# Retention layer: the input projection as seven products per pair of tiles, the attention in items of one head and 256 tokens, the out projection in one piece

## The reference, cut to what matters

```python
q, k, v, g = jnp.split(h @ w_in, ...)            # h 1024x1024, w_in 1024x6144
q, k = rope(q), rope(k) * dk ** -0.5             # 4 heads, dk 256, dv 512
for each chunk of tokens:                        # decay per head
    scores = q k^T * intra
    o      = scores v + (q state) * q_decay
    state  = state * chunk_decay + (k * k_decay)^T v
o = o * rsqrt(mean(o * o) + eps)                 # per head and token
y = (o * silu(g)) @ w_out                        # w_out 2048x1024
```

## Time and profile before

| what | value |
|---|---|
| median of three runs | 2658.11 us |
| the profiled execution's own time | 2658.08 us |
| its span | 2656.2 us |
| PE busy | 2616.3 us, 98% of the span |
| DVE busy | 1378.0 us, 52% |
| POOL busy | 1500.1 us, 56% |
| ACT busy | 869.6 us, 33% |
| granted TensorE clock | 0.998 |
| HBM read, written | 132.81 MB, 5.24 MB |

### The profile page before, as it was taken

One profiled execution on the slowest core, in us unless ns is written; L12 is line 12 of the kernel. 1 busy time (PEld: TensorE's weight loads), 2 busy tenths in 40 slices (PEclk: granted clock), 3 DMA queues, 4 the chain that ended last, 5 costly groups with the idle time before them and its releaser, 6 DMA issues.

```text
span 2656.2 us, 34669 instructions
## 1 busy us (share of the span) xinstructions
PE 2616.3 (98%) x11833; PEld 2159.5 (81%) x11833; DVE 1378.0 (52%) x1740; ACT 869.6 (33%) x1456; POOL 1500.1 (56%) x1334
## 2 busy tenths in 40 slices
PE   8999999999999999999999999999999999999998
PEld 6888888888888788888888788888877888888887
DVE  8333322323325856465563647375678364655644
ACT  4130120121124533333333524234256233333324
POOL 4314323322433478888788644363453788887865
PEclk9999999999999999999999999999999999999999
DMA  4102112111111111211212111111111112112122
GB/s 144 41 28 64 44 32 61 48 36 52 48 44 44 43 54 48 63 47 47 63 53 66 36 49 45 36 56 40 45 56 38 59 48 63 47 47 63 47 68 83
DMA packets 173780, 139.44 MB, mean 52 GB/s; under 512 B 9200, under 2 KB 143472, under 8 KB 173680
## 3 DMA queue, kind: packets, MB, share of 16 engines
q1 hardware_dynamic: 171584, 133.46, 16.8%
q10 hardware_dynamic: 2096, 4.62, 0.5%
HBM read 132.81 MB, written 5.24 MB: 52 GB/s over the span
## 4 chain that ended last, share of the span: by engine, by line
PE 86%; DVE 8%; issue 3%; ACT 2%; DMA 0%; DVEq 0%; SPq 0%; ACTq 0%
PE ps L978 28%; PE ps L982 28%; PE ps L981 28%; DVE residual L2786 2%; DVE f_h_lo L2530 1%; DVE uc L2877 1%; PE ps L1318 0%; DVE h_lo L2326 0%; PE ps L1227 0%; DVE scratch L2307 0%; ACT gate_buf L1628 0%; DVE uc L2871 0%; DVE f_act L2742 0%; DMA residual<-in_x 0%; DVE gate_buf L2882 0%
## 5 line engine op out<-in xcount | busy, mean ns | idle before, releaser
L745 POOL TENSOR_TENSOR f_w_lo<-f_raw,f_w_hi 128x512 fp32r<-128x512 f32 x306 | 434.4, 1423 | 253.1 <-ACT f_w_hi L1837 94.4
L703 POOL TENSOR_TENSOR small<-w_raw 128x1 f32<-128x1 f32 x200 | 54.9, 274 | 792.8 <-PE ps L978 782.3
L978 PE MATMUL ps<-f_h_hi,f_w_hi 128*128 128x512 f32 x1232 | 481.1, 391 | 3.7 <-DVE f_h_lo L2530 2.4
L982 PE MATMUL ps<-f_h_hi,f_w_lo 128*128 128x512 f32 x1232 | 479.6, 389 | 0.0
L981 PE MATMUL ps<-f_h_lo,f_w_hi 128*128 128x512 f32 x1232 | 479.5, 389 | 0.0
L978 PEld LDWEIGHTS ps<-f_h_hi,f_w_hi 128*128 128x128 f32 x1232 | 231.3, 188 | 57.5 <-issue 4.3
L982 PEld LDWEIGHTS ps<-f_h_hi,f_w_lo 128*128 128x128 f32 x1232 | 231.3, 188 | 48.1
L981 PEld LDWEIGHTS ps<-f_h_lo,f_w_hi 128*128 128x128 f32 x1232 | 231.3, 188 | 47.0
L714 POOL TENSOR_TENSOR w_lo<-w_raw,w_hi 128x512 fp32r<-128x512 f32 x190 | 258.7, 1362 | 15.2
L745 POOL TENSOR_TENSOR f_w_lo<-f_sum,f_w_hi 128x512 fp32r<-128x512 f32 x142 | 220.4, 1553 | 60.9 <-ACT f_w_hi L1837 60.9
L978 PE MATMUL ps<-h_hi,w_hi 128*128 128x512 f32 x632 | 249.0, 394 | 0.9 <-DVE h_lo L2277 0.6
(11 more groups left out here) (365 smaller groups left out, 4985.9 us busy)
## 6 DMA issues: line engine op xcount, KB each, us to landing
f_raw<-in_ffn_w_gu SPq DMA_DIRECT2D x176, 256.0 KB, 3.9
w_raw<-in_ret_w_in SPq DMA_DIRECT2D x96, 256.0 KB, 2.8
f_raw<-in_ffn_w_down SPq DMA_DIRECT2D x88, 256.0 KB, 2.9
w_raw<-in_lru_w_in SPq DMA_DIRECT2D x48, 256.0 KB, 2.9
w_raw<-in_ret_w_out SPq DMA_DIRECT2D x32, 256.0 KB, 2.6
w_raw<-in_lru_w_out SPq DMA_DIRECT2D x24, 256.0 KB, 2.8
residual<-in_x SPq DMA_DIRECT2D x8, 512.0 KB, 7.7
out_y<-residual SPq DMA_DIRECT2D x7, 512.0 KB, 2.7
```

Of the source, the lines that this page charges most:

```text
L703: nc.gpsimd.tensor_tensor(small[:, 62:63], col, col, ALU.subtract)
L745: nc.gpsimd.tensor_tensor(lo, src, hi.bitcast(F32), ALU.subtract).then_inc(f_wready, 1)
L978: m = nc.tensor.matmul(o, l_hi, r_hi, start=start, stop=False, skip_group_check=onto)
L982: return nc.tensor.matmul(o, l_lo, r_hi, start=False, stop=stop, skip_group_check=onto)
```

## The change: what it does

The loop over heads goes. In its place:

1. **Norm and first pair.** `norm_by_halves` and `norm_by_halves_act` get a form for `layer == RET` (-1), which makes the seven forms of the normed input right at the start of the program, and `first_products(RET)` does the first two units of the input projection in the order of `PLACES_FIRST`.
2. **Input projection.** 24 units of two 128-feature tiles each (`IN_ORDER`: per head v, v, q, k, and the eight units of g at the end), seven products each, in PSUM banks 0 to 3. All results are features by tokens. DVE turns q and k (`turned`, 12 operations of 128x512 per unit), ACT applies Silu to g; SP writes each unit's four 128x512 parts to HBM (`spill`).
3. **Attention by items.** 16 items (head, 256 tokens), each of four parts, placed between products: part m follows product 35 + 19m/10 (`PARTS`). Part 0: k turned and scores; 1: v turned back to tokens by features; 2: outputs and state; 3: outputs turned. Its operands are read from HBM (`load_qk`, `load_v`), its outputs, normed and turned, are written there (`store_o`). It uses banks 4 to 7.
4. **Out projection.** `load_rows` reads o and g by head and half of the tokens, DVE multiplies, ACT and DVE split; 64 weight pieces, each 12 matmuls, first all of tokens 0 to 511, then 512 to 1023. x is read from HBM again (`x_again`), as `X` serves as work space meanwhile.

The core of it:

```diff
+IN_UNITS = 24
+OUT_UNITS = 64
+IN_ORDER = ([(kind, h, i) for h in range(HEADS) for kind, i in (("v", 0), ("v", 1), ("q", 0), ("k", 0))]
+            + [("g", h, i) for h in range(HEADS) for i in range(2)])
+ITEM_PARTS = 4
+FIRST_PART = 35
+PARTS = {}
+for m in range(ITEM_PARTS * ITEMS):
+    PARTS.setdefault(FIRST_PART + m * 19 // 10, []).append((m // ITEM_PARTS, m % ITEM_PARTS))
...
-            head(0, True)
-            with pe.Fori(1, HEADS - 1) as h:
-                head(h, False)
-            head(HEADS - 1, False, True)
+            for i in range(4):
+                transposes(RET, i)
+            pe.wait_ge(cols_ready, 1)
+            first_products(RET)
+            pe.wait_ge(ident_ready, 3)
+            for r in range(2, IN_UNITS):
+                for p in range(PRODUCTS):
+                    in_product(r, p)
+                    for it, part in PARTS.get(PRODUCTS * r + p, ()):
+                        if part == 0:
+                            keys_and_scores(it)
+                        elif part == 1:
+                            values_turned(it)
+                        elif part == 2:
+                            outputs_and_state(it)
+                        else:
+                            outputs_turned(it)
+            out_rows()
             ffn(0)
```

PE's products of a unit, and what they wait for:

```diff
+            def in_product(r, p):
+                j, form, before = PRODUCTS * r + p, H_OF[p], 0 if r == 2 else r - 1
+                if p == 0:
+                    if IN_ORDER[before][0] in "qk":
+                        pe.wait_ge(r_rope, 12 * turned_no(before) + 2)
+                    else:
+                        pe.wait_ge(r_c11, plain_no(before) + 1)
+                elif p < 4:
+                    pe.wait_ge(f_ev, in_ev(before, (None, E_C21, E_C12, E_T6)[p]))
+                elif p == 4:
+                    pe.wait_ge(f_t, r + 1)
+                else:
+                    pe.wait_ge(f_ev, in_ev(r, (E_T5, E_T7)[p - 5]))
```

```diff
+            def projected():
+                angles()
+                turns(4096.0)
+                whole_turns()
+                for i in range(3):
+                    less(i, 4096.0)
+                first_pair_up()
+                turn_arguments()
+                for r in range(2, IN_UNITS):
+                    turn = IN_ORDER[r][0] in "qk"
+                    for p in range(PRODUCTS):
+                        j = PRODUCTS * r + p
+                        if p in (1, 2, 3):
+                            in_sum(r, p - 1)
+                        elif p == 4 and turn:
+                            turned(r, 0, 2)
+                        elif p == 5:
+                            in_less(r, E_C21, j + 1)
+                            if turn:
+                                turned(r, 2, 6)
+                        elif p == 6:
+                            in_less(r, E_C12, j + 1)
...
+                        if p == 6 and turn:
+                            turned(r, 6, 12)
```

ACT's order at the start, in `norm_by_halves_act(RET)`:

```diff
+                    root(0, 4, turn_a)
+                    for j in range(3):
+                        w_round_first(c, j)
+                    act.wait_ge(cols_ready, 1)
+                    act.wait_ge(n_sq, 4)
+                    for k in FOUR:
+                        from_bank(H_hi[:, h_cut(H_Q11, k)], k)
+                        from_bank(t_q[:, t_cut(k)], k)
+                    for k in FOUR:
+                        from_bank(H_hi[:, h_cut(H_Q21, k)], 4 + k)
+                        from_bank(r3(4 + k), 4 + k)
+                    first_term(c, 0, AT_FIRST)
+                    unit(3)
+                    first_term(c, 1, AT_FIRST)
+                    for s in range(4, SB):
+                        act.wait_ge(x_in[s], 16)
+                        square_rows(s, 0, t_b[:, t_cut(s - 4)])
+                    scaled_last()
```

and DVE's and ACT's work around the first out rows (in unit 23, p counts its products):

```diff
+                        if r == IN_UNITS - 1:
+                            if p in (2, 3):
+                                rows_gated(p - 2)
+                            elif p == 5:
+                                rows_lower(0)
+                rows_lower(1)
...
+            def out_ahead(end, done=[3]):
+                for w in range(done[0], end):
+                    if w in ROWS_AT:
+                        rows_upper(ROWS_AT[w])
+                    out_round(w)
```

More of the change, by code:

```diff
@@ L391, in hn_at @@
         def hn_at(order, what, k, layer):
-            return layer * len(order) + order.index((what, k)) + 1
+            return (layer + 1) * len(order) + order.index((what, k)) + 1
         def h_cut(form, k):
@@ L578, in pair @@
                     for i, src in enumerate(tile_rows_of(f, 1)):
+                        if first and layer == 0:
+                            sp.wait_ge(f_wready, n.units - 4 + i + 1)
                         if not first and i == 0:
@@ new lines, in values_turned @@
+            def values_turned(it):
+                c = it % N_CHUNKS
+                pe.wait_ge(r_vin, 16 * (it + 1))
+                pe.wait_ge(r_mask, it + 1)
+                if c < N_CHUNKS - 1:
+                    pe.wait_ge(r_kt, chunks_before(it) + 1)
+                for blk in range(CHUNK):
+                    for d in range(4):
+                        m = nc.tensor.transpose(bank(4 + blk, d * P, P),
+                                                v_raw[:, d * ITEM + blk * P:d * ITEM + (blk + 1) * P], ident[:])
+                    m.then_inc(r_vt, 1)
@@ L1936, in norm_by_halves_act @@
-                for s in range(4, SB):
-                    added(act, n, 1, s)
-                    square_rows(s, 1, r3(s - 4))
-                root(4, SB, turn_b)
-                act.wait_ge(n_rstd, turn_b)
-                for half in range(2):
-                    for s in (6, 7):
-                        at = s * D + half * 512
-                        nc.scalar.activation(xn_at(half, s), X[:, at:at + 512], ACT.Copy,
-                                             scale=rstd[:, s:s + 1]).then_inc(hx_act, 1)
@@ L1946, in norm_by_halves_act, with junk, scaled_last @@
-                act.wait_ge(n_sq, sq + 16)
-                first_term(c, 0, AT_FIRST)
-                from_sum(H_T1, 0, t_a, "T1")
-                q_12(0)
-                q_12(1)
-                from_sum(H_T1, 1, t_a, "T1")
-                unit(3)
-                first_term(c, 1, AT_FIRST)
+                def junk(s):
+                    return t(s) if s < 3 else dk[:, 0:512]
+                def scaled_last():
+                    root(4, SB, turn_b)
+                    act.wait_ge(n_rstd, turn_b)
+                    for half in range(2):
+                        for s in (6, 7):
+                            at = s * D + half * 512
+                            nc.scalar.activation(xn_at(half, s), X[:, at:at + 512], ACT.Copy,
+                                                 scale=rstd[:, s:s + 1]).then_inc(hx_act, 1)
@@ new lines, in item_turned, with rows_upper @@
+            def item_turned(it):
+                for blk in range(CHUNK):
+                    act.wait_ge(r_ot, 2 * it + blk + 1)
+                    nc.scalar.activation(o_raw[:].rearrange("p (d n) -> p d n", d=4)[:, :, blk * P:(blk + 1) * P],
+                                         bank(4 + blk).rearrange("p (d n) -> p d n", d=4), ACT.Copy).then_inc(r_oc, 1)
+            def rows_upper(q):
+                half, h = divmod(q, HEADS)
+                act.wait_ge(r_gated, q + 1)
+                act.wait_ge(f_mm, PROJECTED + 20 + 4 * h if half else PROJECTED - (0 if h >= 2 else 4))
+                nc.scalar.activation(rows_hi[h][:], o_and_g(q)[0], ACT.Copy).then_inc(r_rh, 1)
@@ L2510, in adds @@
                         e = by_halves(n, nh, half * 4 + i)
-                        add(e, i + (4 * nh if half == 0 else 0), half * 4 + i, nh)
+                        if layer == 0:
+                            out_add(half, nh, i)
+                        else:
+                            add(e, i + (4 * nh if half == 0 else 0), half * 4 + i, nh)
                 def seen(*what):
@@ L2610, in first_tiles_up, with out_rows @@
+            def out_rows():
+                for q in (2, 3):
+                    rows_gated(q)
+                    rows_lower(q)
+                for i in range(4):
+                    out_add(0, 0, i)
+                for q in (4, 5, 6):
+                    rows_gated(q)
+                    rows_lower(q)
+                for i in range(4):
+                    out_add(0, 1, i)
+                rows_gated(7)
+                rows_lower(7)
             def first_tiles_up(layer):
```

1433 lines of the change are left out of this document (789 added, 644 removed).

## The result

The changed kernel takes 2667.59 us (median of 6 runs, 2667.25 to 2669.59). The kernel before took 2657.86 us beside it (6 runs, 2656.07 to 2658.49). The ratio is 1.0039, its 95% interval 1.0026 to 1.0052: slower by 9.7 us, where 11.6 us less was forecast.

The account below looks back on a forecast made before the run. PE was taken to bound the retention layer from end to end. Terms -51.6 + 25.3 + 8 + 6.7 = -11.6 took 2658.1 to 2646.5 us; own range 2636 to 2655, chance 0.50; whole range 2620 to 2675.

Parts of the forecast that it names:

- Products and v turned back: Input projection: 288 fewer matmuls save 64.9 us, 128 more transposes of v cost 13.3; PE's work falls by 51.6 us.
- the split parts' slow pace: Rival, chance 0.10: v transposes at 0.23 us each instead of 0.104 add 12 us net and eat the saving; 2658.
- The start: Norm and first pair: PE waits 42.6 us against 17.3 before in the whole layer; adds 25.3, bounds 10 and 35.
- the walk: Step-by-step timing of the start: T1 at 37.4, (0,6) at 77.3 behind eight angle operations, last products end at 85.3.
- The second rival: q and k units: DVE becomes the bound if two-SBUF-input operations take 1.48 us or more; 2668, chance 0.20.
- The middle: Between the products from unit 2 on: PE waits 8 us over 64 attention parts, bounds 0 and 30.
- 0.7 us of lateness: Attention parts: the longest step is some 0.7 us late behind the four rope operations of product 5.
- From input to out projection: PE waits 3 us for row 0's lower part and 3.7 behind row 2; together 6.7, bounds 0 and 15.
- The clock: Half clock after idling: 1.8 us added for the hole before (0,6); two shorter holes about 1.7 each, not summed.

Follow-up runs that it names:

- POOL almost idle: Changed kernel with POOL's weight sums and lower parts on 32 of 512 columns from unit 2 of the input projection on; 2651.04 us.
- The narrow turning: Changed kernel with each of DVE's 96 rope operations on 32 of 512 columns; 2654.6 us.
- the moved turning: Changed kernel with squares early, angles spread, rows 2 and 3 later, plus each turned unit's last six turning operations put behind the next unit's value parts; 2644.22 us.
- angles behind: Changed kernel with DVE's eight angle operations put behind the sums of the first pair instead of ahead; 2664.61 us.
- row 2 later: Changed kernel with ACT making the upper parts of out projection rows 2 and 3 before weights 7 and 10 instead of 5 and 9; 2661.74 us.
- all four together: Changed kernel with squares early, angles spread, rows 2 and 3 later and the last six turning operations behind the value parts; 2644.22 us.
- the filled kernel: Changed kernel with 45 unread matmuls of 128x512 put in PE's hole before product (0,6) of the first pair; 2663.94 us.

## Why the prediction was wrong

The sign was wrong although each place was named. Two prices of the sum failed: that of DVE's operations beside POOL, in the start and between the products, and that of PE's half clock behind a wait, which was counted once. The sum was -51.6 + 25.3 + 8 + 6.7 = -11.6. Measured by the same parts it is -51.6 + 33.6 + 15.8 + 10.7 + 0.7 = +9.2, beside 9.3 between the spans. The start is 95.44 - 44.5 of work - 17.3 waited before. The middle is 692.04 - 95.44 = 596.6 less a content of 580.8: 22 units' 1848 matmuls and the 432 of values and state at 0.2252, 54.0 of small ones and 13.3 of transposes. The out projection is 879.03 - 692.04 less 768 matmuls and 32 transposes, 176.3. The 0.7 is the FFN pair.

*Products and v turned back: right.* With POOL almost idle the whole middle takes 581.4 us where the content is 580.8, a wait of 1.5 at its end included. The transposes of v run at 8 in 0.79 us, as counted. So the 51.6 us are saved. Of the rivals, the split parts' slow pace is out by the same numbers.

*The start: 33.6 for 25.3.* The step that failed is the price of DVE's operations beside POOL. T1 begins at 42.30 and not at 37.4, by 4.9 us: the four squares took 6.0 us for 3.4, and the four scalings 5.1, where the walk had two, at 0.7 each. The chain of forms from there held to 0.3. The angles and sums took 12.6 us for 10.1, as three short operations counted at 0.75 took 1.63 to 1.79. What lies behind (0,6) is 10.4 us for 9.8. The estimate of 0.75 came from half the columns, and for a copy or a scaling with one input in SBUF no row of before had shown what POOL does to it. The same price was known for two inputs and used only as a bound.

The Trainium skill, "SBUF — State Buffer", section "Who interferes with whom", goes further than the part of it that the prediction used: casts and `tensor_scalar` can enter two-port modes and then contend with GpSimd as well. By that rule each of the three operations beside POOL would have been priced with a wait for one of POOL's, and the trace agrees: 1.63 to 1.79 beside POOL, 0.68 to 0.75 without it.

*The middle: 15.8 for 8.* The second rival named the mechanism and came within 0.4 us of the time, 2668, but that is luck: it gave the middle 30 us where 15.8 were measured, and left the start and the out projection 12.3 us short. Its own condition was not met: it decided from a mean of 1.48 us per operation with both inputs in SBUF, and the mean of the 80 of them is (32.1 + 21.1 + 17.4 + 17.4 + 11.0) / 80 = 1.24. A whole unit of DVE's work does fit. What doesn't is the burst: POOL's operations come in runs, and beside such a run six turning operations took 7.4 us with the item's value part behind them. Averaging over the unit hid this, and so did treating 0.7 us of lateness as a spread over 64 parts. The narrow turning (13.0 less, 12.3 of it in the middle), POOL almost idle (16.6 less, 15.2 of it in the middle) and the moved turning (5.8 less) agree on it. The 15.8 us are 8.7 of waits for DVE, 1.5 of short waits for POOL's weights, 3.1 of slow matmuls behind two of the waits, 1.5 at the end, and 1.0 in small steps.

*From input to out projection: 10.7 for 6.7.* Two waits were forecast, 3 and 3.7 us, and both came, 1.4 and 4.25. The first lies in the middle by the marks used here; with it on this side the out projection is 12.2 and the middle 14.3. The slow stretch behind the second, 1.7 us, was left out; moving row 2 took both away, 5.9 us. Of the 10.7, 5.1 are waits, 1.7 is the slow stretch, and some 4 are left. Of these about 1.2 are a misreading: a matmul in a full row starts 0.2267 us after the last (mean of 219 in the FFN stretch of the earlier trace rows), not 0.2252, since the 222 counted in 50 us take in matmuls that lie across its ends. In the middle the same misreading is more than made up for by the small matmuls, whose time was had by subtraction (2280 x 0.0015 = 3.4 us against 3504 x 0.0015 = 5.3).

*The clock: mis-sized.* One hole was given 1.8 us, and a sentence that two more would cost about 1.7 each stood outside the sum. The start, the middle and the out projection have five holes with a slow stretch: 84.99 (2.3 us more than at full pace), 39.81 (16 transposes in 3.29 us for 1.66, and then five matmuls, 2.7 together), 159.42 (1.6), 455.38 (1.5) and 710.75 (1.7). Filling the first with matmuls gave back about 2.2. That at 39.81 is in part hidden by DVE's chain, which waits 1.45 us for PE at 47.66. The 1.8 us stood in the earlier trace rows and belonged in the sum for each hole that was walked. The rule of "TensorE: Matmul & The Clock Gate", section "What's actually happening" (the Trainium skill), that PE runs at half its clock after an idle stretch, agrees with the row at 84 us, 0.50. The row with 1.00 for the first transposes is no evidence against it: that trace's clock record begins at 18.1 us only, behind them.

What stays open: where the rest of the out projection (about 2.7 us) comes from, and what decides whether a short wait has a slow stretch behind it. The wait of 1.7 us at the first item stands in eleven of the traces and has one in four of them (the changed kernel, angles behind, row 2 later, all four together); the wait of 2.5 us for the values stands in eight and has one in all but the filled kernel's. Some 1.6 us per short wait thus come and go from trace to trace, and with one trace of each kernel the runs don't tell whether the order decides it or the single execution.

## What to carry to other kernels

When a layer is full of one engine's work, a cut of that work uncovers the others: look for each place where the cut leaves the engine nothing beside a serial chain, and price the chain by its slowest rows, with the co-runner that it will have, not by the mean over a unit. Ask of each burst what stands behind it in the same queue; moving an operation past the burst (angles, squares, a row's rounding, the second half of the turning) cost little and gave 23.4 us here, which turned 9.7 us lost into 13.5 won. A removed instruction is worth its slot only where nothing has to wait for the next one.

## What the runs showed of the hardware that was not expected

- A DVE operation with one input in SBUF (copy with conversion, `tensor_scalar`) is held by POOL too: 128x1024 in 1.63 to 1.79 us beside POOL, 0.68 to 0.75 without; a conversion of 128x32 in 1.28 beside it, 0.18 without. Operations with an input in PSUM stayed at 0.69.
- It goes both ways: POOL's 128x512, 1.29 us alone, took 6.14 us for two while DVE worked on 128x2048 (at 707.85).
- PE's granted clock was 0.50 behind waits of 11.5, 7.2, 4.25 and 2.55 us, and this cost 1.5 to 2.7 us on top of each. Behind the wait of 1.69 us at 159.42 it was still 1.00 from 159 to 161 us, with 14 short matmuls, and fell only then: 0.58 from 161 to 163, 1.6 us lost.
